# At most four gathers in flight: a limit on POOL's indirect DMAs in a two-layer decoder kernel

## The reference, cut to what matters

```python
def block(args):
    x_blk, idx_blk, g_blk = args
    hid = jax.nn.gelu(jnp.einsum('td,thkd->thk', x_blk, u_tab[idx_blk]), approximate=False)
    coef = (g_blk * hid.astype(jnp.float32)).astype(x_blk.dtype)
    return jnp.einsum('thk,thkd->td', coef, v_tab[idx_blk])
```

## Time and profile before

| | |
|---|---|
| median of 3 runs | 3632.03 us (3630.02 to 3648.26) |
| span of the profiled execution | 3680.9 us (its time outside the span is not given apart) |
| first gather to last | 228.1 to 3669.8 us |
| POOL, 2048 gathers | 1986.8 us busy, 0.97 us each |
| DVE, 1024 U rows | 1205.0 us busy, 1.22 us each |
| DMA moved | 1247.14 MB, mean 339 GB/s |

### The profile page before, as it was taken

How to read it: one execution, slowest core, us unless ns; L and a number is a source line. 1 busy time by engine, 2 the same in 40 slices (tenths; PEclk the granted TensorE clock), 3 DMA queues, 4 the chain that set the end, 5 groups by cost and what they waited for, 6 DMA issues and landing times.

```text
span 3680.9 us, 29623 instructions
## 1 busy us (share of the span) xinstructions
PE 2077.6 (56%) x9038; PEld 972.8 (26%) x9038; DVE 2235.5 (61%) x5009; ACT 829.9 (23%) x2489; POOL 2002.9 (54%) x2084
## 2 busy tenths in 40 slices
PE   7774575576754475496563446387564356632325
PEld 3532421233312232244221322143331132200001
DVE  3369767475578666845458666837558655558340
ACT  3212313132123122123222121213212212220211
POOL 1024555465557565636457655635646665666665
PEclk9787776787867687798776768688786677755656
DMA  8289799898999899979899879979989889999999
GB/s 258 84 304 361 266 376 334 300 409 318 361 346 358 332 366 386 387 293 366 335 375 359 325 288 406 370 278 372 337 341 357 328 323 349 376 367 372 376 369 344
DMA packets 345853, 1247.14 MB, mean 339 GB/s; under 512 B 39539, under 2 KB 39609, under 8 KB 344417
## 3 DMA queue, kind: packets, MB, share of 16 engines
q0 software_dynamic: 295744, 1075.38, 77.5%
q1 hardware_dynamic: 48656, 160.79, 12.0%
q10 hardware_dynamic: 1296, 9.08, 0.6%
HBM read 1238.90 MB, written 6.20 MB: 338 GB/s over the span
## 4 chain that ended last, share of the span: by engine, by line
DVE 23%; PE 22%; another core or an unknown queue 19%; issue 16%; POOL 9%; DMA 8%; ACT 4%; SPq 0%; DVEq 0%; POOLq 0%; ACTq 0%
PE work L869 10%; DVE ring L1166 9%; POOL ring L483 9%; PE work L839 5%; PE accs L853 4%; DMA ring<-in_peer_u,idxU 3%; PE work L830 2%; DMA ring<-in_peer_v,idxR 2%; DMA wring<-in_w_out 1%; DVE proj L1178 1%; DMA wring<-in_peer_wq 1%; DVE proj L1174 1%; DVE arena L1222 1%; DMA wring<-in_w_in 1%
## 5 line engine op out<-in xcount | busy, mean ns | idle before, releaser
L483 POOL DMA_INDIRECT ring<-in_peer_u,idxU x1024 | 994.0, 971 | 892.6 <-issue 278.9
L1166 DVE CUSTOM_DVE_ANT_0 ring<-ring,n2U 128x1024 f32<-128x1024 f32 x1024 | 1205.0, 1218 | 338.5 <-DMA ring<-in_peer_u,idxU 247.1
L483 POOL DMA_INDIRECT ring<-in_peer_v,idxR x1024 | 992.8, 970 | 743.0 <-issue 276.6
L853 PE MATMUL accs<-ring,wv 128*32 128x512 f32 x4096 | 720.8, 839 | 719.5 <-DMA ring<-in_peer_v,idxR 499.8
L869 PE MATMUL work<-wring,nT 128*128 128x449 f32 (+1 forms) x1152 | 564.3, 626 | 251.9 <-issue 86.8
L853 PEld LDWEIGHTS accs<-ring,wv 128*32 128x32 f32 x4096 | 148.7, 137 | 1206.3 <-issue 1118.5
L869 PEld LDWEIGHTS work<-wring,nT 128*128 128x128 f32 x1152 | 233.6, 210 | 547.8 <-issue 366.5
L547 ACT ACTIVATE wv<-stack,coefR 128x32 f32<-128x32 f32 x1024 | 235.4, 309 | 356.5 <-remote 178.1
L519 ACT ACTIVATE arena<-work 128x512 f32<-128x512 f32 (+3 forms) x208 | 113.2, 563 | 604.7 <-remote 296.1
L869 PE MATMUL work<-wring,n2A 128*128 128x449 f32 x384 | 167.1, 558 | 0.0
L519 ACT ACTIVATE proj<-work 128x512 f32<-128x512 f32 (+1 forms) x88 | 48.9, 577 | 489.0 <-PE work L869 221.6
(11 more groups left out here) (292 smaller groups left out, 2135.5 us busy)
## 6 DMA issues: line engine op xcount, KB each, us to landing
wring<-in_w_in SPq DMA_DIRECT2D x160, 449.0 KB
wring<-in_w_out SPq DMA_DIRECT2D x64, 512.0 KB
wring<-in_peer_wq SPq DMA_DIRECT2D x64, 512.0 KB
ring<-in_peer_u,idxU POOLq DMA_INDIRECT x1024
ring<-in_peer_v,idxR POOLq DMA_INDIRECT x1024
held<-in_peer_wq SPq DMA_DIRECT2D x16, 512.0 KB, 7.2
arena<-keys_scr ACTq DMA_DIRECT2D x8, 1024.0 KB
keys_scr<-ring SPq DMA_DIRECT2D x2, 1024.0 KB, 4.9
```

The costliest lines, as they stand in the source:

```text
L483: nc.gpsimd.indirect_dma_start(ring[:, s * D:(s + 1) * D], None, table, bass.IndirectOffsetOnAxis(ap=idx, axis=0)).then_inc(row_in[s], 16)
L853: ins = nc.tensor.matmul(acc[c][quarter(r), :], wv[:, d * QUARTER:(d + 1) * QUARTER], ring[:, s * D + 512 * c:s * D + 512 * c + 512], star ...
L1166: V.tensor_tensor_reduce(out=rw, in0=rw, in1=n2U[:], scale=1.0, scalar=0.0, op0=ALU.mult, op1=ALU.add, accum_out=hid[:, kk:kk + 1]).then_i ...
```

## The change

A constant FLIGHT = 4 is added. Before it issues row r, POOL waits until row r - 4 has landed in full (semaphore `row_in` of its slot). The wait is in addition to those for the slot and for the numbers.

```diff
 QUARTER = P // UNIT
 WBUFS = 4
+FLIGHT = 4
 AHEAD = 2
@@ def gather(table, idx, row)
             def gather(table, idx, row):
                 s = row % SLOTS
+                if row >= FLIGHT:
+                    pool.wait_ge(row_in[(row - FLIGHT) % SLOTS], row_count(row - FLIGHT))
                 nc.gpsimd.indirect_dma_start(ring[:, s * D:(s + 1) * D], None, table, bass.IndirectOffsetOnAxis(ap=idx, axis=0)).then_inc(row_in[s], 16)
```

## The result

| | before | limit of four |
|---|---|---|
| median | 3632.45 us (3630.02 to 3648.26, 4 runs) | 3796.59 us (3786.50 to 3799.43, 4 runs) |
| ratio to before | | 1.044, 95% interval 1.040 to 1.048 |
| span of the profiled execution | 3680.9 us | 3784.4 us (its time 3786.5 us) |

The change costs 164 us.

The account below looks back on a forecast made before the run. No engine was full, so waits decided, the path alternating over DVE, PE and gathers; 0.22 us more per gather, counted as 129 or 77 us, gave 100 us, or 99 on the 3632 us median: 3731, rounded to 3735, range 3640 to 3880.

Parts of the forecast that it names:

- the forecast's case: Gathers under the limit: a pace of 1.35 to 1.55 us and a rise of 30 to 160 us, chance 0.58.
- rival C: Gather-bound, POOL bounding the kernel: landings stay at 5.9 us, pace 1.61 us, 218 us lost, time 3847 us; chance 0.20.
- What bounds: No engine full; path over DVE, PE and gathers by turns; POOL's 899.4 us of slot waits cover slower gathers.
- w, 0.26 and up to 0.85 us: POOL's wake-up after a landing: 0.26 us with a single wait, up to 0.85 behind a separate semaphore instruction; 0.54 taken.
- L, 5.3 us: A gather's time from start of issue to landing, expected to fall from 5.9 us toward 4.54 under the limit.
- The pace, 1.46 us: Interval between POOL's gathers with four in flight, (5.3 + 0.54)/4 = 1.46 us, 0.22 more than now.
- The share that lands, 588 or 352 gathers: Gathers whose 0.22 us delay is paid: 588 by bursts (129 us), 352 by POOL's chain share (77 us); middle 100 us.
- The last 281 us, 10 to 40 us: The kernel's end, 188 gathers and little else: 10 to 40 us of the loss should fall there.
- Weight stretches lose nothing: Where weights load, DMA engines are full and stay full with four gathers in flight, so nothing should be lost.
- Rival A: The limit does not bind, or DMA bandwidth is the true limit: time stays at 3632 us within 18; chance 0.13.
- the burst count: 168 places where users catch up with POOL, times 3.5 gathers, half a burst of 7.0: 588 late gathers.
- Rival B: Faster: short gather queues let weights through, saving about 59 us of PE's 118.6 us weight waits, time 3573; chance 0.09.

Follow-up runs that it names:

- w4: Limit four only at the 558 of 2048 rows issued while weights are loaded, all other gathers as in the kernel before; 3655.69 us, ratio 1.005.
- the kernel with one memset: The kernel before, no limit on gathers in flight, with one small memset on POOL behind each gather to space them; ratio 1.001.

## Why the prediction came out as it did

The direction and the range held: 3796.59 us lies in 3640 to 3880, 62 us above the forecast of 3735. The rise was 164 us where 30 to 160 were given to the forecast's case, so the result stands at the border to rival C. The signs that the prediction had named say more: gathers that wait were to stand 1.4 to 1.55 us apart and the chain's landings to take 4.6 to 5.6 us, and both came out above; a pace over 1.6 us with POOL hardly ever waiting for a slot was the sign of C, and that is what the trace shows (1.67 us at the end, 106.5 us of slot waits). The mechanism is the one forecast, at the strength of C. By its steps:

- **What bounds.** Right. POOL's slot waits were the cover, they went, and PE and DVE then waited for gathers at 225 + 427 places instead of 168.
- **w, 0.26 and up to 0.85 us.** Right in kind and size: 0.26 and 0.72 were measured. It is the term whose share is best shown, since moving it alone gave back 102 us.
- **L, 5.3 us.** The step that failed: "L should fall from the mean of the five (5.9) toward 4.54". It did not fall. The chain after shows 5.96, 5.97 and 6.69 us, and a median of 6.11. Only limit three brought it to 5.3.
- **The pace, 1.46 us.** Too low for that reason. With 6.11 us and 0.72 or 0.26 the formula gives 1.71 or 1.59 us; the last 281 us ran at 1.67, stalls included. The rise for a closely spaced gather was thus about 0.43 us over the 1.24, twice the 0.22 that I had set.
- **The share that lands, 588 or 352 gathers.** The middle of the two counts, 455 gathers at 0.22 us, made 100 us. With 0.43 us the 164 us answer to 381 gathers, so the middle was too high and the rise too low. The two errors worked against each other, and that luck is why the total was only 62 us off. That the chain's count (352) came near is luck too, for the number of gathers that land on the path is no constant of the kernel. With the waits in the other order the pace is (6.1 + 0.26)/4 = 1.59 us, 0.35 more than before, and the loss is 55 us: 157 gathers. With three it is 0.76 more and 775 us: 1020 gathers. As I read it, POOL's waits for slots cover the first tenths of a microsecond, and what comes on top is paid for at more and more gathers; the counts rest on the formula's paces, and the cover itself was not measured. The prediction took one count for every loss of pace.
- **The last 281 us, 10 to 40 us.** 188 gathers at 1.67 instead of 1.49 us are 34 us.
- **Weight stretches lose nothing.** Nearly: share 0.99 at 656 us, and limit four there alone costs 0.5%; the stretches themselves took 1151 us there against 1094 without the limit, and 17 us show in the time. The prediction had the engines full in all of these stretches before; between 700 and 740 us, with weight loads under way, the DMA share was 0.82.
- **Rival A** is out by every row. **Rival C** had the mechanism right, POOL waits for slots fell from 899.4 to 106.5 us and the pace was its 1.61 us, but its price of 218 us used the burst count and was too high. (The time at its far end, 365 us over 3632, is 3997 us and not 3990.) **Rival B** saw rightly that PE's waits for weights would go, 118.6 to 26.2 us, one of the signs that the prediction had set against itself, and wrongly that this would be worth time: w4 has it and is no faster.

The Trainium skill's fit ("DMA: Bandwidth & Descriptors", Anatomy of one DMA), by which a gather would take 3.2 us, an estimate from its figures, and the limit never bind, is not borne out: over all runs the quickest gather on a chain took 4.03 us (at 3593.74 us in the run of limit five with the waits in the other order), and the median with limit four was 6.11 us.

What stays open: why limit five was 1.5% faster. It was measured on one chip, against 13 runs of the kernel before. The shorter waits for weights are in it, but w4 has them without a gain; limit five with the waits in the other order, on another chip, has neither them nor more than 0.6% of gain. The weave of gathers and other work is written out by hand for one timing, and another timing may fit it better by chance; nothing here shows it. Limit five on the chip of the last session was not tried, so whether it would be a better kernel in general is not known.

## What to carry to other kernels

A limit on transfers in flight is a limit on pace: landing time plus wake-up, divided by the number, must stay below the interval at which the issuer can and must issue. Read the landing time under load off the chain, and do not count on it to fall because fewer are in flight. Where an instruction has two waits, let the one that usually ends last sit on the instruction itself; with four in flight that gave back 102 us here, with five nothing. To price a slower stream, do not multiply by a fixed number of gathers: how many of them are paid for grows with the loss of pace, from 157 to 1020 here.

## What the runs showed of the hardware that was not expected

- A wake-up behind a separate semaphore instruction took 0.72 us on POOL, and 0.26 us where the DMA instruction carried the wait.
- The landing time of a 512 KB gather on the chain was 6.11 us with four in flight (median of 343), about the 5.2 to 6.6 us of before, and 5.34 us with three (median of 570).
- PE waited at most 0.6 us for a wq piece with gathers limited to four or five, and up to 15.9 us without a limit on the first chip. On the chip of the last session it waited at most 0.6 us without a limit too.
- Two chips differ by 11% on this kernel, 3639 against 3236 us for the kernel before. On the faster one the kernel with one memset moved 404 to 411 GB/s in 30 of the 40 slices of its span, which its page shows below, and 385 GB/s on average, where the kernel before moved 339 GB/s on average in its profile on the first chip. The cause is not known.

```profile
GB/s 243 87 237 409 288 408 409 409 409 404 394 409 393 409 405 409 409 408 400 409 410 409 371 405 409 409 408 409 408 409 405 381 406 409 409 409 409 411 409 362
```
